# Row maxima of dilated attention from rounded 64-row operands, the two heads of a pair in turn

## What is computed

```python
def dilated_window_attention(q, k, v, window, dilation):
    # per residue class of the dilation: own block of keys and the one before
    s = jnp.einsum('brhcqe,brhcke->brhcqk', qb, kb) * (E ** -0.5)
    s = jnp.where(valid, s, -jnp.inf)
    m = jnp.max(s, axis=-1)
    p = jnp.exp(s - m[..., None])
    l = jnp.sum(p, axis=-1)
    o = jnp.einsum('brhcqk,brhcke->brhcqe', p, vb)
    return back(o), back(m), back(l)
...
ms = jnp.stack(maxes)
wts = jnp.exp(ms - jnp.max(ms, axis=0))
den = jnp.sum(wts * jnp.stack(dens), axis=0)
num = jnp.sum(wts[..., None] * jnp.stack(outs), axis=0)
o_b = (num / den[..., None]).reshape(B, S, ATT_DIM) * jax.nn.silu(ag.astype(jnp.float32))
```

## Time and profile before

| | |
|---|---|
| median of the runs | 1509.21 us (1509.03 to 1509.48) |
| the profiled execution's own time | 1508.62 us |
| its span, first to last instruction | 1506.5 us |
| PE, matmuls | 1488.2 us busy (99%), 7927 instructions |
| PEld, weight loads | 1271.6 us (84%) |
| DVE | 854.9 us (57%) |
| ACT | 705.1 us (47%) |
| POOL | 33.3 us (2%) |
| DMA queue of SP | 115.94 MB, 24.1% of the 16 engines |
| mean granted TensorE clock | 0.999 |

### The profile page before, as it was taken

How to read it: one execution, slowest core, us unless ns; L and a number is a source line. 1 busy time by engine, 2 the same in 40 slices (tenths; PEclk the granted TensorE clock), 3 DMA queues, 4 the chain that set the end, 5 groups by cost and what they waited for, 6 DMA issues and landing times. The chain is left out here.

```text
span 1506.5 us, 21102 instructions
## 1 busy us (share of the span) xinstructions
PE 1488.2 (99%) x7927; PEld 1271.6 (84%) x7927; DVE 854.9 (57%) x1387; ACT 705.1 (47%) x877; POOL 33.3 (2%) x39
## 2 busy tenths in 40 slices
PE   7999999999999999999999999999999999999998
PEld 5888888888888888888888888888888888888987
DVE  6646555473646374667952586358635865644523
ACT  6646565665647474745522434344334435411212
POOL 1000000000000000001400000000000000000000
PEclk9999999999999999999999999999999999999999
DMA  5121111121111211122313212321232134332702
GB/s 217 43 70 57 53 46 69 56 70 56 53 58 56 70 45 66 56 70 71 89 53 87 68 36 79 86 70 33 81 85 70 31 105 135 118 119 100 263 29 84
DMA packets 35520, 116.84 MB, mean 78 GB/s; under 512 B 6200, under 2 KB 6520, under 8 KB 35448
## 3 DMA queue, kind: packets, MB, share of 16 engines
q1 hardware_dynamic: 35456, 115.94, 24.1%
HBM read 83.21 MB, written 20.02 MB: 69 GB/s over the span
## 5 line engine op out<-in xcount | busy, mean ns | idle before, releaser
L682 PE MATMUL z_ps<-h_hi,w_hi 128*128 128x512 f32 x1392 | 551.3, 396 | 0.6 <-ACT zz L1172 0.6
L684 PE MATMUL z_ps<-h_hi,w_lo 128*128 128x512 f32 x1392 | 542.8, 390 | 0.0
L683 PE MATMUL z_ps<-h_lo,w_hi 128*128 128x512 f32 x1392 | 542.2, 390 | 0.0
L684 PEld LDWEIGHTS z_ps<-h_hi,w_lo 128*128 128x128 f32 x1392 | 261.3, 188 | 55.6
L682 PEld LDWEIGHTS z_ps<-h_hi,w_hi 128*128 128x128 f32 x1392 | 261.7, 188 | 52.1 <-issue 1.6
L683 PEld LDWEIGHTS z_ps<-h_lo,w_hi 128*128 128x128 f32 x1392 | 261.8, 188 | 50.4
L1322 DVE TENSOR_TENSOR w_lo<-w_stage,w_hi 128x1024 fp32r<-128x1024 f32 x89 | 109.4, 1230 | 225.7 <-ACT w_hi L1012 225.2
L1020 ACT ACT_TABLE_LOAD x61 | 78.3, 1283 | 77.7 <-PE z_ps L684 77.0
L1120 ACT ACTIVATE pt<-pb 128x512 f32<-128x512 f32 (+1 forms) x80 | 43.4, 543 | 119.5 <-PE pb L828 119.2
L1012 ACT ACTIVATE w_hi<-w_stage 128x1024 fp32r<-128x1024 f32 x89 | 93.8, 1054 | 0.3
L845 PE MATMUL pc<-pt,vb 128*128 128x128 f32 x560 | 77.6, 279 | 1.2 <-ACT pt L1120 1.2
(11 more groups left out here) (257 smaller groups left out, 2202.6 us busy)
## 6 DMA issues: line engine op xcount, KB each, us to landing
w_stage<-w_in SPq DMA_DIRECT2D x88, 512.0 KB, 3.4
z_swap<-zz SPq DMA_DIRECT2D x96, 128.0 KB, 2.3
gate_d<-gate SPq DMA_DIRECT2D x16, 512.0 KB, 4.3
x_in<-x SPq DMA_DIRECT2D x8, 512.0 KB, 7.6
o_a_d<-o_a SPq DMA_DIRECT2D x8, 512.0 KB, 4.7
w_stage<-w_a SPq DMA_DIRECT2D x8, 512.0 KB, 3.8
cos_t<-gate_d SPq DMA_DIRECT2D x8, 512.0 KB, 4.6
sin_t<-gate_d SPq DMA_DIRECT2D x8, 512.0 KB, 3.6
```

The lines of the kernel that those rows point to most:

```text
L682: nc.tensor.matmul(z_ps[hf][:], w_hi[s][:, k, :], h_hi[:, k, t], start=k == 0, stop=False)
L683: nc.tensor.matmul(z_ps[hf][:], w_hi[s][:, k, :], h_lo[:, k, t], start=False, stop=False)
L684: last = nc.tensor.matmul(z_ps[hf][:], w_lo[s][:, k, :], h_hi[:, k, t], start=False, stop=k == KT - 1)
```

## The change

`maxima` now issues both heads' matmuls of a block one after the other, each from 64 rows. For groups 0 and 1 these are the rounded halves of `q_two` and `k_two`, rows 64h to 64h+63. For group 2 they are rounded too: ScalarE rounds q into the other 64 rows of the other head's `q_sh[2]` (slot 14), and k into a new tile `k_hi2`, which lies where `zz1` is (slot 14, ahead of the denominators). So that q can be written there, VectorE forms its sum in one add in `zz0` at the end of slot 11, and SP copies it to `q_sh[2]` by two DMAs behind the swap of k. Before it writes v into `zz0`, ScalarE waits for these two DMAs. Since the 64 spare rows of `q_sh[2]` are now written in each pair, GpSimd clears nothing there; `k_sh[2]` has zeros in those rows. All four matmuls of a part wait until the row maxima of both heads of the part before are done (of two parts before in pair 0).

```diff
             def rows_to_queries(i):
 
+                if first(i):
+                    sp.wait_ge(padded, PADS)
...
+                        if c == 6:
...
+                            if prev:
...
+                                sp.wait_ge(st_made, scored)
+                            for h in range(2):
+                                rows = slice(EDIM * h, EDIM * (h + 1))
+                                sp.dma_start(q_sh[2][h][rows, :].bitcast(f32), zz[0][rows, :]).then_inc(q2_copied, 16)
...
-            def maxima(i, g, m, h):
-
-                u = 2 * (g * 4 + m) + h
-                if first(i):
-                    if u >= 4:
-                        pe.wait_ge(mx_taken, max_count(u - 3))
-                elif max_bank(i, g, m) is pc:
+            def maxima(i, g, m):
+
+                u = 2 * (g * 4 + m)
+                if max_bank(i, g, m) is pc and not first(i):
                     pe.wait_ge(ob_taken, i * N_SUMS)
-                elif u >= 2:
-                    pe.wait_ge(mx_taken, i * N_MAX + max_count(u - 1))
+                elif not first(i):
+                    pe.wait_ge(mx_taken, i * N_MAX + max_count(u))
+                elif u >= 4:
+                    pe.wait_ge(mx_taken, max_count(u - 2))
+                if g == 2:
+                    pe.wait_ge(g2_rounded, i * 4 + 4)
                 else:
-                    pe.wait_ge(mx_taken, i * N_MAX)
...
-                    pe.wait_ge(qk_lo_done, i * 4 + 2 * g + 2)
-                    pe.wait_ge(q_dupped, i * 4 + 2 * g + h + 1)
-                for blk, at, before in max_queries(g, m):
+                    pe.wait_ge(qk_hi_done, i * 8 + 4 * g + 4)
+                todo = max_queries(g, m)
+                for blk, at, before in todo:
                     lo = blk - 1 if before else blk
                     at += 0 if before or g == 2 else P
-                    q_side, k_side = (q_two[g][h], k_two[g][h]) if g < 2 else (q_sh[2][h], k_sh[2][h])
-                    last = nc.tensor.matmul(max_bank(i, g, m)[:, h, at:at + P * (blk + 1 - lo)], q_side[:, P * blk:P * blk + P],
-                                            k_side[:, P * lo:P * blk + P], start=True, stop=True)
-                last.then_inc(mx_made, 1)
+                    for h in range(2):
+                        rows = slice(EDIM * h, EDIM * (h + 1))
+                        q_side, k_side = (q_two[g][h], k_two[g][h]) if g < 2 else (q_sh[2][1 - h], k_hi2)
+                        last = nc.tensor.matmul(max_bank(i, g, m)[:, h, at:at + P * (blk + 1 - lo)], q_side[rows, P * blk:P * blk + P],
+                                                k_side[rows, P * lo:P * blk + P], start=True, stop=True)
+                        if blk == todo[-1][0]:
+                            last.then_inc(mx_made, 1)
...
+                    if cur and slot == 14:
+
+                        act.wait_ge(q2_copied, i * 32 + 32)
+                        for h in range(2):
+                            rows = slice(EDIM * h, EDIM * (h + 1))
+                            nc.scalar.activation(q_sh[2][1 - h][rows, :], q_sh[2][h][rows, :].bitcast(f32), ACT.Copy).then_inc(g2_rounded, 1)
...
                             if g == 0 and hf == 0:
-                                act.wait_ge(rope_sum, i * 6 + 5)
+                                act.wait_ge(q2_copied, i * 32 + 32)
...
+                    if cur and slot == 14:
+
+                        act.wait_ge(rope_sum, i * 6 + 6)
+                        for h in range(2):
+                            rows = slice(EDIM * h, EDIM * (h + 1))
+                            nc.scalar.activation(k_hi2[rows, :], k_sh[2][h][rows, :], ACT.Copy).then_inc(g2_rounded, 1)
...
-                        if j < 4:
+                        if j < 5:
                             nc.vector.tensor_tensor(zz[j % 2][:], zz[j % 2][:], z_swap[:], ALU.add).then_inc(rope_sum, 1)
```

More of the change, by code:

```diff
@@ L194, in place_side @@
         def place_side(name, g, h):
[L196 removed]
+            sides[name][g][h] = place(f"{name}{g}{h}", [P, SEQ], f32 if (name, g) == ("k_sh", 2) else f32r)
         for name, g, h in (("q_two", 0, 0), ("q_two", 1, 0), ("q_two", 0, 1), ("q_sh", 0, 0), ("q_sh", 0, 1), ("q_two", 1, 1), ("q_sh", 1, 0),
@@ L201, in build @@
             place_side(name, g, h)
-        zz = [place(f"zz{s}", [P, SEQ]) for s in range(2)]
+        zz = [place("zz0", [P, SEQ])]
+        zz1_at = top[0]
+        zz.append(place("zz1", [P, SEQ]))
         z_swap = place("z_swap", [P, SEQ])
@@ L215, in build @@
         m_rows = place("m_rows", [2, GROUPS, SEQ])
+        top[0] = zz1_at
+        k_hi2 = place("k_hi2", [P, SEQ], f32r)
         s_ag, o_b, v_t = z_swap, r_den, zz[0]
@@ L827, in scores_t @@
                         nc.tensor.matmul(dst, k_two[g][h][:, ks], q_two[g][h][:, qs], start=False, stop=False)
-                    last = nc.tensor.matmul(dst, k_sh[g][h][:, ks], q_sh[g][h][:, qs], start=False, stop=blk == units[-1][0])
+                    q_side = q_sh[g][h][:, qs] if g < 2 else q_sh[g][h][:, qs].bitcast(f32)
+                    last = nc.tensor.matmul(dst, k_sh[g][h][:, ks], q_side, start=False, stop=blk == units[-1][0])
                 last.then_inc(st_made, 1)
@@ L877, in attention @@
                         for g, m in MAX_SLOTS.get(slot, ()):
-                            for h in range(2):
-                                maxima(i, g, m, h)
+                            maxima(i, g, m)
                     if cur and slot == 17:
@@ L1592, in attention @@
                                 row_max(i, g, m, h)
-                    if cur and slot in (12, 14):
-                        j = (slot - 4) // 2
-                        dve.wait_ge(rope_a, i * 6 + j + 1)
-                        dve.wait_ge(rope_b, i * 6 + j + 1)
+                    if cur and slot == 14:
+                        dve.wait_ge(rope_a, i * 6 + 6)
+                        dve.wait_ge(rope_b, i * 6 + 6)
                         if prev:
@@ L1601, in attention @@
                             rows = slice(EDIM * h, EDIM * (h + 1))
-                            dst = (q_sh, k_sh)[j % 2][2][h]
-                            last = nc.vector.tensor_tensor(dst[rows, :], zz[j % 2][rows, :], z_swap[rows, :], ALU.add)
+                            last = nc.vector.tensor_tensor(k_sh[2][h][rows, :], zz[1][rows, :], z_swap[rows, :], ALU.add)
                         last.then_inc(rope_sum, 1)
```

30 lines of the change are left out of this document (12 added, 18 removed).

## The result

| | before | after |
|---|---|---|
| median of the runs (us) | 1509.03 (1507.91 to 1510.14, 15 runs) | 1512.78 (1511.33 to 1513.61, 15 runs) |
| profiled execution, its span (us) | 1508.62, 1506.5 | 1512.91, 1510.8 |
| TensorE busy | 1488.2 us | 1484.5 us |

The ratio of the times is 1.0023, with an interval from 1.0016 to 1.0030: the changed kernel is 3.75 us slower. 1510.8 us had been forecast.

What follows compares the result with a forecast made beforehand. TensorE was taken as the bound; -6.9 (group 2) + 4.2 (slot 12) - 0.7 (slot 14) + 3.4 (transpose) + 1.5 (pair 0) = +1.5 us, so 1510.8 us, called no change; range 1504 to 1517.

Steps and rivals of the forecast that it cites:

- What bounds the kernel: Whole kernel: TensorE, busy 1488.2 of 1506.5 us; only its own time or its waits can move the end.
- VectorE, slot 12: Pairs 1 to 3: the add ahead of the row maxima starts the projection 1.4 us later each, 4.2 us in all.
- Slot 14 of pairs 1 to 3: Earlier k rotation removes a wait for row maxima: 0.3 us less in pairs 1 and 2, 0.1 in pair 3.
- ScalarE and the transpose of slot 17: Pairs 1 to 3: two k copies lengthen the chain to 20.45 us; 3.4 us of gain lost at the transpose.
- SP and the take of slot 12: q copies by DMA delay ScalarE's take: 1.5 us of new wait in pair 0, hidden in pairs 1 to 3.
- Matmuls of the maxima: Row maxima matmuls: 0.115 us each, nothing saved in groups 0 and 1; group 2 1.72 us less per pair, 6.9 total.
- rival 1: Small matmuls: the halves overlap, each four save 0.23 us, group 2 another 0.9; 1506 us, chance 0.24.
- rival 2: Maxima bursts: 37 changes between whole and half array at 0.2 us cost 7.4 us; 1518 us, chance 0.20.
- Rival 3: VectorE and ScalarE catch up, so the waits do not form: -7.6 us, 1502 us, chance 0.12.
- rival 4: SP's q copies land 2 us later than worked out in all pairs: +2.9 us, 1514 us, chance 0.08.

Runs made afterwards that it cites:

- x_bank: Changed kernel with the maxima of slot 12 of pairs 1 to 3 written into the PSUM tensor of the scores: 1508.9 us.
- y_kl2: Changed kernel with ScalarE's two k roundings moved from slot 14 to slot 16, behind the weight split: 1507.44 us.
- x_klate: Changed kernel with ScalarE's two k roundings moved from slot 14 to the end of slot 15's list, landing just ahead of the weight split: 1512.42 us.
- x_first: Changed kernel with SP's two copies of the group 2 q sum issued ahead of the four swaps instead of behind them: 1511.28 us.
- z_addlate: Changed kernel with VectorE's one add for q of group 2 put back at slot 12, behind the row maxima of slot 11: 1525.27 us.
- x_apart: Changed kernel with head 0's matmuls of a part all ahead of head 1's instead of in turn: 1512.29 us.
- experiment 4: Changed kernel with groups 0 and 1 from all 128 rows again, group 2 still at 64; run twice: 1512.71 and 1511.35 us.
- y_best: Changed kernel, k roundings behind the weight split, q copies ahead of swaps, slot 12 maxima in scores' PSUM tensor, groups 0 and 1 from 128 rows: 1497.49 us.

## Why the prediction was right, and where it was wrong

No change was forecast, with a small loss of 1.5 us. The loss is 3.75 us, 0.23% by the ratio, inside the range, and its interval (0.16 to 0.30%) lies on both sides of the 0.2% that was named as the bound. That it came so close is in part luck: two errors of 2.6 and 3.3 us in the price of the maxima have opposite signs. Step by step:

- **What bounds the kernel**: right. Every loss and gain was one of TensorE's intervals or waits.
- **VectorE, slot 12**: forecast +1.4 us a pair, measured 1.03, 1.08 and 1.13. The wait is as described, a little shorter; x_bank showed that it hangs on the single bank.
- **Slot 14 of pairs 1 to 3**: forecast -0.7, measured -0.3. The wait did go, but a switch took part of the gain.
- **ScalarE and the transpose of slot 17**: the length of the chain was right (20.56 against 20.55 us), and with it the net of group 2 and the transposition: -0.6 a pair forecast, -0.59, -0.59 and -0.89 measured (in pair 2 the shift against before goes from 3.94 to 3.35 us). y_kl2 showed that the two copies are the whole of what came back. x_klate showed what the step didn't say: moved elsewhere in the same chain they cost as much.
- **SP and the take of slot 12**: forecast 1.5, measured 1.5; x_first removed it whole. In pairs 1 to 3 it was hidden, as forecast, and z_addlate shows how thin that cover is.
- **Matmuls of the maxima**: this is the step that failed, in both halves. "If each keeps paying 0.115 us, 64 rows instead of 128 and the alternation of heads save nothing" is wrong: the heads run at the same time. "I take 0.115 and no switching price" is wrong too. The two errors nearly cancel in a burst of four (+0.14 to +0.19 us, where 0 was taken) and not in one of sixteen (-2.38, where -1.72 was taken). From the forecast to the ledger that is -2.6 us in group 2 and +3.3 in the other bursts. But group 2's further gain ran into the wait ahead of the transposition, which ScalarE and VectorE set, and 1.6 us of it came back there (+5.0 instead of +3.4). Slots 12 and 14 give -1.0 and +0.4, the small steps +0.3: 2.0 us together, from 1.5 to 3.5.
- **The rivals**: rivals 1 and 2 were argued as alternatives, and each is true in part. The heads overlap, but four matmuls save 0.03 to 0.04 us and not rival 1's 0.23; only group 2, with 0.8 us where 0.9 was said, goes as it says. The changes have a price, 0.09 us in and 0.11 to 0.13 out, about half of the 0.2 that rival 2 put on each, but most of the 72 cost it and not 37. So rival 2's aside, "or 1513 if the halves overlap", came within 0.2 us with terms that are off and cancel; that both effects could be there together deserved a chance of its own. The two rules of the Trainium skill that were weighed (TensorEngine Tiling (Array Packing), Key Properties: different tiles load and run in parallel; a change of tiling mode drains TensorE) both bear on what came. With the first this case's trace agrees, by starts 3 to 4 ns apart. With the second it agrees so far that a change has a price, 318 ns instead of 227; whether that is a drain no run here shows. The argument against them, that every small matmul of the trace sat at 0.11, was one from rows that all used the whole array.
- Rival 3 fell (all waits formed); rival 4 fell (the copies landed when forecast).

## What to carry to other kernels

Going from the whole array to two half arrays and back cost 0.2 to 0.33 us here. The first and the last couple of a burst gain almost nothing, and each couple of 128 columns between them saves 0.12 us (110 ns instead of two steps of 115), so by these numbers about eight matmuls are needed before it pays (an estimate: 0.16 to 0.19 us lost with two couples, 0.12 won back by each further one). With 256 columns a further couple saves only 0.01 to 0.02 us (223 ns instead of 233 to 240), and by the same estimate it doesn't pay at all at such lengths. Two unknown effects that point in opposite directions can both be true, and that case belongs among the forecasts. And an operation that is added to an engine with time to spare is priced by what stands behind it in that engine's list, up to the next thing that the bound engine waits for: moving two copies, six DMAs and one bank was worth 10.8 us. And waits of 2 us on the bound engine are worth removing for a second reason, the clock behind them.

## What was not expected of the hardware

- **Matmuls of the other half overtake.** In x_apart the second half's first matmul started 6 ns behind the first half's first, ahead of one that stood before it in the list. So the starts recorded here are not in the order of the list once the two halves of the array are used; with the kernel's own interleaved list the starts are 3 to 4 ns apart.
- **The overlap depends on the columns.** Couples of 128 columns follow one another every 109 to 114 ns in group 2, couples of 256 columns every 223, hardly less than two single ones on the whole array (233 to 240). The forecast had "64, 128 and 256 columns cost about the same", which held for the whole array only.
- **Waits can cost more than themselves.** Behind an idle time of 1.83 us the granted clock fell to its lower level for 3.4 us in one execution of experiment 4's kernel and stayed at full in another; that cost 1.6 us on top of the wait. In z_addlate it fell at idle times of 2.31, 2.91 and 3.32 us and not at one of 2.23, at 6.6 us in all. In the changed kernel, whose longest wait in the attention is 1.5 us, it stayed at full there in the profiled execution.
- **The same program starts in two ways.** In five of thirteen profiles TensorE ran at full speed 15 us into the program, in eight at half speed, and the eight reached the attention 0.6 to 1.8 us later.

Not tried: a form in which VectorE writes the q sum straight to the tile that the maxima read, so that the two DMAs go; and y_best with the add of slot 12 at other places. Open: why some executions start at half speed for longer than others.
